# Norms by token chunk between the additions, the next run's first weight tile split ahead, and an embedding's products moved between the halves of its gate

## The reference, cut to what matters

```python
h = x
for layer in range(DEPTH):                       # DEPTH = 2
    hn = rmsnorm(h, norm_mix[layer])
    if layer % 2 == 0:
        h = h + even_mixer(hn, ...)              # recurrence + state-space mixer
        h = h + swiglu(rmsnorm(h, norm_ffn[layer]), ffn_w_gu[j], ffn_w_down[j])
    else:
        h = h + s5_mixer(hn, ...)                # ends in a GLU
        h = h + moe_swiglu(rmsnorm(h, norm_ffn[layer]), w_router, ...)
    gate = sigmoid(rmsnorm(h, norm_ple[layer]) @ ple_gate[layer])
    h = h + gate * (p[layer] @ ple_proj[layer])  # per-layer embedding
return rmsnorm(h, final_norm)

def rmsnorm(x, w):
    return x * rsqrt(mean(x * x, axis=-1) + 1e-6) * w
```

## Time and profile before

| | us |
|---|---|
| median of 3 runs (2748.8 to 2751.13) | 2749.0 |
| the profiled execution's own time | 2751.23 |
| its span, first to last instruction | 2749.3 |
| PE busy | 2512.3 (91%) |
| DVE busy | 1707.1 (62%) |
| ACT busy | 1254.6 (46%) |
| POOL busy | 232.7 (8%) |
| mean granted TensorE clock | 0.956 of full |

### The profile page before, as it was taken

How to read it: one execution, slowest core, us unless ns; L and a number is a source line. 1 busy time by engine, 2 the same in 40 slices (tenths; PEclk the granted TensorE clock), 3 DMA queues, 4 the chain that set the end, 5 groups by cost and what they waited for, 6 DMA issues and landing times.

```text
span 2749.3 us, 31447 instructions
## 1 busy us (share of the span) xinstructions
PE 2512.3 (91%) x12526; PEld 2010.3 (73%) x12526; DVE 1707.1 (62%) x2010; ACT 1254.6 (46%) x1400; POOL 232.7 (8%) x240
## 2 busy tenths in 40 slices
PE   4989888889999997969869999999999999999977
PEld 2445464458888785758759988998889988998853
DVE  5697797532222324395347678767887688667852
ACT  2343333122222222455226567656765677656741
POOL 3012854200000000000000000000000000000010
PEclk9999989899999998989959999999999999999989
DMA  8545610122322222435056789877997799777950
GB/s 237 142 145 168 180 62 31 39 69 92 104 96 92 92 92 77 138 135 192 19 185 236 256 298 380 283 254 257 374 336 251 254 324 375 263 256 268 376 194 31
DMA packets 316338, 526.14 MB, mean 191 GB/s; under 512 B 19238, under 2 KB 175498, under 8 KB 313530
## 3 DMA queue, kind: packets, MB, share of 16 engines
q1 hardware_dynamic: 287114, 479.73, 50.5%
q0 software_dynamic: 5888, 25.78, 3.0%
q10 hardware_dynamic: 23184, 18.55, 2.1%
HBM read 494.46 MB, written 45.81 MB: 197 GB/s over the span
## 4 chain that ended last, share of the span: by engine, by line
PE 79%; DVE 11%; ACT 3%; POOL 3%; issue 2%; DMA 1%; ACTq 0%; DVEq 0%; POOLq 0%
PE psum L1768 26%; PE psum L1350 16%; PE psum L1827 12%; PE psum L1608 6%; PE psum L1829 5%; PE psum L1245 4%; PE psum L1268 3%; PE psum L1419 1%; POOL stages L1071 1%; DVE stages L834 1%; POOL stages L1074 1%; DVE stages L844 1%; PE psum L1222 1%; DVE stages L839 1%; DVE stages L835 1%
## 5 line engine op out<-in xcount | busy, mean ns | idle before, releaser
L3192 DVE TENSOR_TENSOR stages_r<-kept,stages_r 128x2048 fp32r<-128x2048 f32 x336 | 769.1, 2290 | 243.5 <-ACT stages_r L2305 242.6
L2305 ACT ACTIVATE stages_r<-kept 128x2048 fp32r<-128x2048 f32 x336 | 637.2, 1912 | 230.8 <-PE psum L1768 104.2
L1768 PE MATMUL psum<-stages_r 128*128 128x512 f32 x3136 | 738.8, 394 | 3.2 <-issue 3.2
L1768 PEld LDWEIGHTS psum<-stages_r 128*128 128x128 f32 x3136 | 583.7, 188 | 127.1 <-issue 4.8
L1827 PE MATMUL psum<-stages_r 128*128 128x320 f32 x1792 | 465.5, 345 | 6.3 <-issue 3.2
L1350 PE MATMUL psum<-stages_r 128*128 128x512 f32 x1920 | 440.7, 392 | 11.4 <-DVE stages_r L2867 11.4
L1350 PEld LDWEIGHTS psum<-stages_r 128*128 128x128 f32 x1920 | 363.5, 189 | 87.9 <-issue 11.8
L1829 PE MATMUL psum<-stages_r 128*128 128x160 f32 x1792 | 423.4, 236 | 0.0
L2867 DVE TENSOR_TENSOR stages_r<-kept,stages_r 128x2048 fp32r<-128x2048 f32 x54 | 123.6, 2293 | 361.9 <-ACT stages_r L2165 361.9
L1829 PEld LDWEIGHTS psum<-stages_r 128*128 128x128 f32 x1792 | 343.3, 192 | 2.0
L1827 PEld LDWEIGHTS psum<-stages_r 128*128 128x128 f32 x1792 | 337.4, 188 | 9.0 <-DVE stages_r L3192 3.8
(11 more groups left out here) (399 smaller groups left out, 2466.7 us busy)
## 6 DMA issues: line engine op xcount, KB each, us to landing
kept<-in_moe_w_gu_dram SPq DMA_DIRECT2D x224, 1024.0 KB, 6.4
kept<-in_moe_w_down_dram SPq DMA_DIRECT2D x112, 1024.0 KB, 6.3
kept<-in_ffn_w_gu_dram SPq DMA_DIRECT2D x28, 1024.0 KB, 5.1
kept<-in_ev_w_in_dram SPq DMA_DIRECT2D x16, 1024.0 KB, 6.4
kept<-in_ffn_w_down_dram SPq DMA_DIRECT2D x14, 1024.0 KB, 5.0
s_output_maps_by_state<-stages ACTq DMA_DIRECT2D x64, 128.0 KB, 2.0
s_input_maps<-stages ACTq DMA_DIRECT2D x32, 256.0 KB, 2.5
s_output_maps<-s_output_maps_by_state SPq DMA_DIRECT2D x32, 256.0 KB, 4.7
```

The costliest lines, as they stand in the source:

```text
L1768: m = pe.matmul(out_, a, b, start=start and n == 0, stop=stop and n == len(pairs) - 1, skip_group_check=True)
L2305: act.activation(w_high[n % WSLOTS], unit_tile(n), ACT.Copy).then_inc(s_wh, 1)
L3192: dve.tensor_tensor(w_low[n % WSLOTS], unit_tile(n), w_high[n % WSLOTS], ALU.subtract).then_inc(s_ws, 1)
```

## The change

1. **Norms by chunk.** `norm` on DVE becomes `scale(k, c)` for one chunk and `turned(k)`; on ACT it becomes `square(k, c)` and `root(k, c)`. Each chunk gets its own square root and reciprocal. For norms 1, 2, 4 and 5, DVE scales chunk c-1 right behind the addition to chunk c; norm 6's squares of chunks 0 to 2 stand between the last four sigmoids, and their one root behind them. PE turns chunks 0 and 1 of norms 1 and 4 before the last additions are done; the order of the PSUM banks is turned by two chunks for that (`TURN_BANK`), and norms 2 and 4 write `hn` at places of their own (`hn2`, `hn4`).
2. **The square root's table** is brought in ahead of norms 2, 4 and 5 by a root that nothing reads (`root_table`).
3. **The first weight tile** of runs 0 and 1 is split before the norm, not behind it. The first tile's low-part products stand last in each bank, and PE waits for the last two low parts only in front of them.
4. **The first embedding**: its input is loaded when the first hidden tile of the feed-forward's second half is split; it is turned behind the gate's first tile and multiplied behind the second, between `pg00` and `pg01`, in banks 0 to 3 and then 4 to 7. DVE multiplies the first half with the gate straight from PSUM.
5. **The second embedding**: its input is turned behind the router's products, and `h` is added to in halves, the first one under the products of `pg11`.

```diff
+        TURN_BANK = lambda c: 2 * ((c + 2) % TC)
+        hn4 = sbuf[:, base:base + 4 * D].rearrange("p (c n) -> p c n", c=4)
+        hn2 = sbuf[:, un_at:un_at + 4 * D].rearrange("p (c n) -> p c n", c=4)
+        hn_of = lambda k: {2: hn2, 4: hn4}.get(k, hn)
+        def rms_done(k, c):
+            return 4 * NTH[k] + (c + 1 if k != 6 else 1 + (c == TC - 1))
...
-            pool.wait_ge(s_ffd, 8)
+            pool.wait_ge(s_ws, hidden_split_count(0))
             pool.dma_start(ptok, p_in[0, 0].rearrange("(c p) n -> p c n", p=P)).then_inc(s_p, 16)
...
+            def turn_chunk(k, c):
+                pe.wait_ge(s_hn, 4 * NTH[k] + c + 1)
+                for g in range(2):
+                    for q in range(4):
+                        m = pe.transpose(psum[:, TURN_BANK(c) + g, q * P:(q + 1) * P],
+                                         hn_of(k)[:, c, (4 * g + q) * P:(4 * g + q + 1) * P], ident)
+                    m.then_inc(s_tp, 1)
+            def transpose_norm(k, parts=False):
                 for c in range(TC):
+                    turn_chunk(k, c)
                 pe.wait_ge(s_hA, 4 * (TURN[k] + 1))
-                pe.wait_ge(s_hD, 4 * (TURN[k] + 1))
+                pe.wait_ge(s_hD, 4 * TURN[k] + (2 if parts else 4))
...
+                    terms = ((f_high, hn_high), (f_low, hn_high), (f_high, hn_low))
+                    order = [(k, n) for k in range(4) for n in range(3)]
+                    if run < 2 and t == 0:
+                        order = [(k, n) for k in range(4) for n in range(2)] + [(k, 2) for k in range(4)]
                     for b in range(4):
                         cols = slice(b * P, (b + 1) * P)
+                        for k, n in order:
+                            if run < 2 and t == 0 and b == 0 and (k, n) == (0, 2):
+                                pe.wait_ge(s_hD, 4 * (TURN[run + 1] + 1))
+                            w, a = terms[n]
+                            pair = (w[kk][:, k, cols], a[:, 4 * kk + k, :]) if layout == "T" else (
+                                a[:, 4 * kk + k, cols], w[kk][:, k, :])
+                            m = pe.matmul(psum[:, 4 * (g % 2) + b, :], *pair, start=kk == 0 and k == 0 and n == 0,
+                                          stop=kk == 1 and k == 3 and n == 2, skip_group_check=True)
...
+                    if t in behind:
+                        behind[t]()
...
+            all_drained("o0")
+            turn_chunk(1, 0)
+            turn_chunk(1, 1)
             all_drained("o1")
-            transpose_norm(1)
+            turn_chunk(1, 2)
+            turn_chunk(1, 3)
+            pe.wait_ge(s_hA, 4 * (TURN[1] + 1))
+            pe.wait_ge(s_hD, 4 * TURN[1] + 2)
             split_product(0)
...
+            def embed_bank(w, pT_, bank, c, hf):
+                for k in range(2):
+                    m = pe.matmul(psum[:, bank, :], pT_[:, k, c * P:(c + 1) * P], w[:, k, hf * 512:(hf + 1) * 512],
+                                  start=k == 0, stop=k == 1)
+                m.then_inc(s_pp, 1)
+            def first_embed():
+                w = tile(ple_tile)
+                pe.wait_ge(s_pTd, 1)
                 for c in range(TC):
+                    embed_bank(w, pT, c, c, 0)
+                all_drained("pg00")
                 for c in range(TC):
+                    embed_bank(w, pT, 4 + c, c, 1)
+                pe.wait_ge(s_ppd, 4)
             pe.wait_ge(s_fd, 8)
-            embed_inputs(0)
-            embed(0)
+            transpose_norm(2, parts=True)
+            split_product(1, {0: lambda: embed_inputs(0, 0), 1: first_embed})
             pe.wait_ge(s_ppd, 8)
-            transpose_norm(2)
-            split_product(1)
-            all_drained("pg00")
...
+            all_drained("gg1")
+            turn_chunk(4, 0)
+            turn_chunk(4, 1)
             all_drained("go1")
-            embed_inputs(1)
-            transpose_norm(4)
+            turn_chunk(4, 2)
+            turn_chunk(4, 3)
+            pe.wait_ge(s_hA, 4 * (TURN[4] + 1))
+            pe.wait_ge(s_hD, 4 * (TURN[4] + 1))
             pe.matmul(psum[:, 1, 128:256], ones, LT, start=True, stop=True)
             pe.matmul(psum[:, 1, 64:65], LT, ones[:, 0:1], start=True, stop=True)
...
             m.then_inc(s_lg, 1)
+            embed_inputs(1, 6)
             pe.wait_ge(s_hot, 2)
...
+            def square(k, c):
+                h_ready[k](act, c)
+                act.activation(hn_of(k)[:, c, :], h[:, c, :], ACT.Square, accum_out=stat[:, k, 0, c:c + 1]).then_inc(s_sq, 1)
+            def root(k, c, n=1):
+                act.wait_ge(s_sq, 4 * NTH[k] + c + n)
+                act.activation(stat[:, k, 1, c:c + n], stat[:, k, 0, c:c + n], ACT.Sqrt, bias=eps, scale=1.0 / D).then_inc(s_rms, 1)
+            def root_table():
+                act.activation(stat[:, 3, 2, 0:1], eps, ACT.Sqrt)
+            def norm(k, parts=False):
                 for c in range(TC):
-                    ready(act, c)
-                    act.activation(hn[:, c, :], h[:, c, :], ACT.Square, accum_out=stat[:, k, 0, c:c + 1]).then_inc(s_sq, 1)
-                act.wait_ge(s_sq, 4 * (NTH[k] + 1))
-                act.activation(stat[:, k, 1, :], stat[:, k, 0, :], ACT.Sqrt, bias=eps, scale=1.0 / D).then_inc(s_rms, 1)
+                    square(k, c)
+                    root(k, c)
...
-            norm(1, h_ready[1], parts=True)
             split_tile(0, 0)
+            norm(1, parts=True)
             split_tile(0, 1)
...
                         split_tile(0, EARLY + 2 * (j - 1) + t)
+            act.wait_ge(s_ffd, 4)
+            split_tile(1, 0)
+            root_table()
+            norm(2, parts=True)
+            split_tile(1, 1)
             act.wait_ge(s_pT, 1)
             act.activation(pT[:, 0, :], psum[:, 0, :], ACT.Copy).then_inc(s_ac, 1)
-            norm(2, h_ready[2], parts=True)
-            split_tile(1, 0)
-            split_tile(1, 1)
...
-            act.wait_ge(s_pT, 2)
-            act.activation(pT1[:, 0, :], psum[:, 0, :], ACT.Copy).then_inc(s_ac, 1)
-            norm(4, h_ready[4])
+            root_table()
+            norm(4)
             act.wait_ge(s_hot, 1)
             act.activation(gate[:, 2, :], gate[:, 0, :], ACT.Exp).then_inc(s_gexp, 1)
+            act.wait_ge(s_pT, 2)
+            act.activation(pT1[:, 0, :], psum[:, 6, :], ACT.Copy).then_inc(s_ac, 1)
...
+            root_table()
             for c in range(TC):
...
-            norm(5, h_ready[5])
-            gate_ple(1)
-            norm(6, h_ready[6], False)
+            norm(5)
+            gate_sigmoids(1, 0)
+            gates, g = pgate[1], gidx["pg11"]
+            for b in range(4):
+                act.wait_ge(s_grp, 4 * g + b + 1)
+                act.activation(gates[:, b, 512:1024], psum[:, 4 * (g % 2) + b, :], ACT.Sigmoid).then_inc(s_drA, 1)
+                if b:
+                    square(6, b - 1)
+            root(6, 0, 3)
+            square(6, 3)
+            root(6, 3)
...
+            def scale(k, c):
+                dve.wait_ge(s_rms, rms_done(k, c))
+                if c == 0:
+                    dve.wait_ge(s_nw[k % 2], 16 * NW_LOADS[k])
+                chain.link(dve.reciprocal(stat[:, k, 2, c:c + 1], stat[:, k, 1, c:c + 1]))
                 chain.settle()
+                dve.scalar_tensor_tensor(out=hn_of(k)[:, c, :], in0=h[:, c, :], scalar=stat[:, k, 2, c:c + 1],
+                                         in1=nw[:, k % 2, :], op0=ALU.mult, op1=ALU.mult).then_inc(s_hn, 1)
...
+            for c in range(TC):
+                scale(0, c)
+            turned(0)
...
-            norm(1, parts=True)
+            for b in range(4):
+                add_to_h("o0", 0, b)
             split_tile(0, 0)
+            for b in range(4):
+                add_to_h("o1", 1, b)
+                if b:
+                    scale(1, b - 1)
+            scale(1, 3)
+            turned(1, parts=True)
             split_tile(0, 1)
...
+            split_tile(1, 0)
             for c in range(TC):
...
                     dve.tensor_tensor(hh, hh, psum[:, 2 * c + hf, :], ALU.add).then_inc(s_fd, 1)
+                if c:
+                    scale(2, c - 1)
+            scale(2, 3)
+            turned(2, parts=True)
+            split_tile(1, 1)
...
+            embed_input(0, 0)
...
             split_tile(1, 2)
-            split_tile(1, 3)
+            def first_half(c):
+                at = slice(0, 512)
+                dve.wait_ge(s_drA, cumA[gidx["pg00"]] - 3 + c)
+                dve.wait_ge(s_pp, c + 1)
+                dve.tensor_tensor(pp[:, c, at], psum[:, c, :], pgate[0][:, c, at], ALU.mult).then_inc(s_ppd, 1)
+                dve.wait_ge(s_ppd, c + 1)
+                dve.tensor_tensor(h[:, c, at], h[:, c, at], pp[:, c, at], ALU.add).then_inc(s_ph, 1)
+            def second_parts():
                 for c in range(TC):
+                    dve.wait_ge(s_pp, TC + c + 1)
+                    dve.tensor_copy(pp[:, c, 512:1024], psum[:, 4 + c, :]).then_inc(s_ppd, 1)
```

(29 more changed lines are left out.)

120 lines of the change are left out of this document (36 added, 84 removed).

## The result

The changed kernel takes **2702.1 us** (median of 4 runs, 2700.4 to 2703.2), the kernel before 2748.9 beside it: a ratio of 0.982, 95% interval 0.981 to 0.984. That is 46.8 us less; 49 were forecast. The profiled execution took 2702.5 with a span of 2700.5, 48.8 less than the span of before.

The account below looks back on a forecast made before the run. PE, 79% of the chain of waits, was taken as the bound, with time won at norms between products. Terms 3.1 + 10.3 + 19.2 + 12.7 + 1.5 + 2.4 = 49.2 gave 2749.0 - 49 = 2700.0 us, range 2692 to 2712.

Parts of the forecast that it names:

- Norm 1: Between mixer and feed-forward: scaling chunks under PE's products and splitting the tile ahead starts PE 8.2 us earlier, plus 2.1 clock: 10.3.
- Norm 2 and the embedding: From last down product to gate's end: early load, moved embedding and chunked norm end the gate at 1121.0, not 1140.2: 19.2 us.
- Norm 4 and the router: Behind the GLU: shorter norm and embedding turned later win 11.2 us, the router's faster products 1.5: 12.7 together.
- the sign to look for: What the new profile should show at the router: it starts within 6 us of the GLU's end.
- The router's term: The router's 64 short products: PE comes to them warmer, winning between nothing and 4.4 us, taken as 1.5.
- Norm 0: At the kernel's start: first scaling no longer waits for three more squares, PE starts at about 34.3, not 37.43: 3.1 us.
- Norm 5: Behind the experts: scalings between additions start PE at 2677.0, not 2679.20; a slow start may return up to 2: 1.5 us.
- Norm 6: Last norm, behind the last sigmoid: less work left, so scalings end at 2743.5, not 2745.9: 2.4 us.
- The clock gave nothing back: Rival at the seams of norms 1, 2, 5 and router: slow starts stay, gain 41.7, time 2707 us; chance 0.20.
- No transfer was late: Rival at the router: its weights, asked for after the last addition, make PE wait 7 us, time 2707; chance 0.05.
- The tile was there: Rival at two seams: tile 0 not in the ring, ACT stands before the norm, 4.2 us back each, 2708; chance 0.02.
- PE was not held at the lower clock: Rival: short pieces keep PE at 1.2 GHz far into the next run, kernel slower, 2760 after 300 products; chance 0.02.

## Why the prediction was right

**Norm 1** (10.3, measured 10.1). ACT's high parts end the wait, the first products start on two chunks of low parts with 0.26 us of waiting behind them, and there is no slow start. The run with the scalings behind and that with the tile behind say that three scalings in the shadow are 2.9 of it and the tile ahead 5.4.

**Norm 2 and the embedding** (19.2, measured 19.1). 6.95 to the first product and 59.05 from there to the gate's end; 7.2 and 58.7 were worked out. Its parts were tested, though not all in the same kernel: load 6.7, place 6.0, of which half is the clock, the tile 3.5; the norm by chunk is what is left.

**Norm 4 and the router** (11.2 and 1.5, measured 10.7 and 1.6). The first was 0.5 too high. Its step "eight transposes (1.07) and a copy (0.7)" behind the last scaling was mis-sized: VectorE has four copies there, one behind the other, and PE waits for the last of them. The router comes 7.5 us behind the GLU's end, where the sign to look for was 6 (the forecast's own sum gives 6.4).

```profile
1332.05 2.48 DVE L2488 COPY stages<-psum 128x512 f32<-128x512 f32 x4
```

The router's term was right by luck: the step "PE comes to them warmer, so between nothing and 4.4 is won" fell. The router takes 9.9 us in a trace with the old order and 13.8 in one with the new.

**Norm 0** (3.1). The two profiles show 1.8 at PE's start and 0.7 at the mixers' last stage; the run with the old order of roots shows 3.3 at PE's start, and all the traces of the old and the new norm 0 are 2.9 apart there on average. So the size of the term was right, though not in the pair of profiles: that of before had the shortest way of the four old ones to the mixers' last stage.

**Norm 5** (1.5, measured 0.8). The step that failed is "three scalings now stand between them, so the last is done at 2674.3 and not at 2676.4". The 2.1 is there, but from the roots by chunk; the place of the scalings brings nothing. The slow start, which I put down to the single transposes, stands in two of the six traces with the new order (56.9 and 57.0) and in none of the five with the scalings behind, nor in the three of the old norm. That fits the forecast's reason, but so few traces don't show it.

**Norm 6** (2.4, measured 2.8). 8.4 us from the last sigmoid's end to the last scaling's, 8.5 worked out; the rest lies in the writing of the output.

**Rivals.** The clock gave nothing back at norms 1 and 2; the run with the tiles behind shows that it would have (0.8 and 2.2 us) had PE stood for 6 us. No transfer was late: PE waits nowhere for the router's weights. The tile was there. PE was not held at the lower clock. One reading against that rival was wrong all the same: that each slow start of before ended within some 4 us. At norm 1 it took 4.0, but at norm 2 5.7, with 13 products of 0.43 or more.

**What I had not seen** is 3.3 us in the mixers' last stage, and 0.6 lost in the S5 mixer. The first is a slow start in the profile of before that nine of fourteen traces don't have, in stretches that the change leaves alone; it can account for the spans' differing by 2 us more than the medians. The cause of the 0.6 stays open: other traces have 220.0 with the new code.

That the sum of the profiles came so close (48.8 for 49.2) is in part luck: these 3.3 us stand in for the 2.4 that this pair lacks at norm 0. What was forecast for norms 1, 2, 4 and 6 is 43.1 and measured 42.7, and there the mechanism was right in the main.

## What to carry to other kernels

In a norm between two products, let each chunk's root follow its own square: the first scaling then waits for nothing else, and where the scalings stand matters only if the vector engine has gaps between its additions. Work that a product needs and that does not depend on the norm (a load, a weight tile's split) belongs ahead of it; the tile's split undone in the finished kernel cost 11.5 us where it brought 6.7 in the old one, mostly because the early start on half of the low parts goes with it, and in part because TensorE's longer stands bring slow starts. Compare such changes by stretches of the trace, as the runs' medians carry 2 to 3 us of slow starts that come and go.
